# A three-layer transformer block on one core: scans spread over the weight stream, layer norm in eight units, features laid out ahead

## The reference

```python
def conformer_conv(h, w_in, dw, dw_b, ln_g, ln_b, w_out):
    a, b, z = jnp.split(h @ w_in, 3, axis=-1)
    v = a * jax.nn.sigmoid(b)
    v = depthwise_conv(v, dw, 31 taps, pad 15) + dw_b
    v = jax.nn.silu(layer_norm(v, ln_g, ln_b))
    return (v * jax.nn.silu(z)) @ w_out

def hgrn_direction(q, k, v, log_f):          # for each head, state carried over chunks of 64
    b = jnp.cumsum(fb, axis=2)
    decay = jnp.exp(jnp.where(lower_tri, b[t] - b[s], -jnp.inf))
    scores = jnp.einsum("bhtk,bhsk,bhtsk->bhts", qb, kb, decay)
    ...                                      # o_intra + o_inter, new_state

def hgrn2_mixer(h, w_in, lb_fwd, lb_bwd, o_norm, w_out):
    q, a_f, a_b, i, z = jnp.split(h @ w_in, 5, axis=-1)
    # forget(a, lb): log_f = log(lb + (1-lb) sigmoid(a)), key = (1-lb) sigmoid(-a)
    o = rms_norm(forward(q, k_f, i, lf_f) + backward(q, k_b, i, lf_b), o_norm)
    return (o * jax.nn.silu(z)) @ w_out
# x = x + conformer_conv(rms_norm(x)); x = x + hgrn2_mixer(rms_norm(x))
# x = x + sliding_window_attention(rms_norm(x)); x = x + swiglu(rms_norm(x))
```

## Time and profile before

| | us |
|---|---|
| median of 3 runs (2176.8 to 2177.96) | 2177.4 |
| the profiled execution | 2176.5 |
| its span | 2174.7 |
| TensorE busy | 2044.6 (94%) |
| VectorE busy | 1244.8 (57%) |
| ScalarE busy | 1067.7 (49%) |
| GpSimd busy | 241.6 (11%) |
| mean granted TensorE clock | 0.975 |

### The profile page before, as it was taken

One profiled execution on the slowest core, in us unless ns is written; L12 is line 12 of the kernel. 1 busy time (PEld: TensorE's weight loads), 2 busy tenths in 40 slices (PEclk: granted clock), 3 DMA queues, 4 the chain that ended last, 5 costly groups with the idle time before them and its releaser, 6 DMA issues.

```text
span 2174.7 us, 26997 instructions
## 1 busy us (share of the span) xinstructions
PE 2044.6 (94%) x9552; PEld 1687.3 (78%) x9552; DVE 1244.8 (57%) x1678; ACT 1067.7 (49%) x1353; POOL 241.6 (11%) x108
## 2 busy tenths in 40 slices
PE   4999997999898989979999897899999999999999
PEld 4777776888686878868788776788888888888887
DVE  1199975454676857578656663454544454544443
ACT  4444445445656666666455563354444444433332
POOL 3888860000000000000000000000000000000000
PEclk9999999999999999999999997899999999999999
DMA  4665562565344444433556332356656665655654
GB/s 153 187 178 182 177 193 75 167 203 180 121 135 145 137 134 135 146 116 123 183 179 202 97 100 76 123 183 191 191 174 199 194 185 182 195 189 187 190 187 155
DMA packets 182189, 350.71 MB, mean 161 GB/s; under 512 B 11548, under 2 KB 11932, under 8 KB 182044
## 3 DMA queue, kind: packets, MB, share of 16 engines
q1 hardware_dynamic: 180608, 348.17, 51.6%
q10 hardware_dynamic: 1478, 1.23, 0.2%
HBM read 347.26 MB, written 2.10 MB: 161 GB/s over the span
## 4 chain that ended last, share of the span: by engine, by line
PE 84%; DVE 6%; ACT 5%; issue 2%; DVEq 1%; ACTq 1%; DMA 1%; POOL 1%
PE acc L362 25%; PE acc L363 25%; PE acc L364 25%; PE T L477 3%; PE T L344 2%; ACT w_hi L640 1%; DVEq L974 1%; DVE w_lo L982 1%; DMA cy<-in_hgrn_lb_bwd_dram 1%; ACTq L650 1%; PE T L556 1%; POOL w_lo L331 1%; DVE Xc L1113 0%; PE T L565 0%; PE T L567 0%
## 5 line engine op out<-in xcount | busy, mean ns | idle before, releaser
L982 DVE TENSOR_TENSOR w_lo<-raw,w_hi 128x1024 fp32r<-128x1024 f32 x560 | 677.2, 1223 | 655.0 <-ACT w_hi L640 648.5
L640 ACT ACTIVATE w_hi<-raw 128x1024 fp32r<-128x1024 f32 x656 | 683.3, 1058 | 560.5 <-PE acc L364 532.0
L362 PE MATMUL acc<-w_hi,h_hi 128*128 128x512 f32 x1888 | 752.5, 399 | 48.1 <-DVE w_lo L982 36.5
L363 PE MATMUL acc<-w_lo,h_hi 128*128 128x512 f32 x1888 | 741.5, 393 | 0.0
L364 PE MATMUL acc<-w_hi,h_lo 128*128 128x512 f32 x1888 | 740.9, 392 | 0.0
L362 PEld LDWEIGHTS acc<-w_hi,h_hi 128*128 128x128 f32 x1888 | 358.4, 190 | 131.0 <-DVE w_lo L982 40.3
L364 PEld LDWEIGHTS acc<-w_hi,h_lo 128*128 128x128 f32 x1888 | 358.0, 190 | 76.3
L363 PEld LDWEIGHTS acc<-w_lo,h_hi 128*128 128x128 f32 x1888 | 358.5, 190 | 70.9
L331 POOL TENSOR_TENSOR w_lo<-raw,w_hi 128x1024 fp32r<-128x1024 f32 x96 | 228.0, 2400 | 68.8 <-ACT w_hi L640 68.7
L1037 DVE SCALAR_TENSOR_TENSOR T<-vpad,feat,T 128x256 f32<-128x256 f32 x464 | 183.6, 481 | 0.7 <-DVE T L1037 0.7
L362 PE MATMUL acc<-w_hi,y_hi 128*128 128x512 f32 x384 | 159.2, 415 | 20.3 <-DVE y_lo L987 11.3
(11 more groups left out here) (197 smaller groups left out, 1398.0 us busy)
## 6 DMA issues: line engine op xcount, KB each, us to landing
raw<-in_hgrn_w_in_dram SPq DMA_DIRECT2D x160, 512.0 KB, 4.3
raw<-in_conv_w_in_dram SPq DMA_DIRECT2D x96, 512.0 KB, 4.2
raw<-in_ffn_w_gate_dram SPq DMA_DIRECT2D x88, 512.0 KB, 4.4
raw<-in_ffn_w_up_dram SPq DMA_DIRECT2D x88, 512.0 KB, 3.9
raw<-in_ffn_w_down_dram SPq DMA_DIRECT2D x88, 512.0 KB, 4.7
raw<-in_attn_w_qkv_dram SPq DMA_DIRECT2D x40, 512.0 KB, 4.2
raw<-in_conv_w_out_dram SPq DMA_DIRECT2D x32, 512.0 KB, 4.8
raw<-in_hgrn_w_out_dram SPq DMA_DIRECT2D x32, 512.0 KB, 4.7
```

What stands on the lines that cost most here:

```text
L362: nc.tensor.matmul(o, hi[:, kt, a], w_hi[:, slot, kk, :], start=kt == 0, stop=False)
L363: nc.tensor.matmul(o, hi[:, kt, a], w_lo[:, slot, kk, :], start=False, stop=False)
L640: A(w_hi[:, slot, :, :], raw[:, slot, :, :], ACT.Copy).then_inc(hi_ready, 1)
L982: TT(w_lo[:, slot, :, :], raw[:, slot, :, :], rounded(w_hi[:, slot, :, :]), ALU.subtract).then_inc(split_ready, 1)
```

## The change

Three things are changed at once.

1. The feature table and x are also given in a turned layout, channels on partitions. `feat` is one load of 128 rows, and x comes in a second time, turned, as four loads into `xT` (the place of `szt`), each before one of the first four weight loads; the ordinary x is loaded behind them. The turns of features and of x at the start are gone. VectorE instead of GpSimd makes `w_lo` for the first 16 chunks.
2. Layer norm: the taps of both halves of a group use one PSUM bank; the mean is summed in two parts at hooks 14 and 27 of `conv_z`, the variance in four parts at hooks 28 to 31. `z_turn(3)` goes behind the second chunk of `conv_out`. The four units become eight units of two blocks; three are begun at hook 3, the others one per hook at hooks 4 to 9, and TensorE waits for unit c before chunk c.
3. Scan passes: the undecayed level comes first, behind TensorE's chunk 7; the forward scans stand at VectorE's hook 8, the backward ones at 9, the two key operations at 10 and 11, the first differences at 12, and the later differences one chunk behind the weighting before them instead of at once behind it. `turn` of the third projection and `gates` are one or two chunks earlier.

```diff
+FIRST_LOWS = 2 * CPG
...
+            def turned_in(k):
+                sp.dma_start(xT[:, 4 * k:4 * k + 4, :], t["x_turned"][:, 4 * k:4 * k + 4, :]).then_inc(xT_in[k], 16)
...
+            def ab(j):
+                at = Hooks()
+                if is_first(j):
+                    for k in range(4):
+                        at.put(k, lambda k=k: turned_in(k)).put(4 + k, lambda k=k: x_rows_in(k))
...
-            for n in range(ph["conv_out"].chunk0):
+            pool.wait_ge(split_ready, FIRST_LOWS)
+            for n in range(FIRST_LOWS, ph["conv_out"].chunk0):
...
+            def mean(q0, q1):
+                pe.wait_ge(c_tap, q1 * GROUP_TAPS)
+                for kt in range(4 * q0, 4 * q1):
+                    last = nc.tensor.matmul(T[:, 3, 0:S], ones[:, :], cy[:, kt, :], start=kt == 0, stop=kt == KT - 1)
                 last.then_inc(c_mean, 1)
...
+            def variance(q):
+                pe.wait_ge(c_sq, q + 1)
+                for i in range(4):
+                    last = nc.tensor.matmul(T[:, 2, 0:S], ones[:, :],
+                                            (atok, fg)[q % 2].rearrange("p a (b c) -> p (a b) c", c=S)[:, i, :],
+                                            start=q == 0 and i == 0, stop=q == 3 and i == 3)
+                last.then_inc(c_var, 1)
             at = Hooks().put(5, lambda: v_turn(3))
...
+            at.put(14, lambda: mean(0, 3)).put(27, lambda: mean(3, 4))
+            for q in range(4):
+                at.put(28 + q, lambda q=q: variance(q))
             stream("conv_z", 0, h_hi, h_lo, at)
-            z_turn(3)
-            mean()
-            variance()
-            stream("conv_out", 0, y_hi, y_lo, x_turns("conv_out", 1, (c_zc, 8)), lambda c: pe.wait_ge(c_lo, c // 2 + 1))
+            stream("conv_out", 0, y_hi, y_lo, x_turns("conv_out", 1, (c_zc, 8)).put(1, lambda: z_turn(3)),
+                   lambda c: pe.wait_ge(c_lo, c + 1))
...
-                at = Hooks().put(0, lambda: turn(j, 0, qtok)).put(1, lambda: turn(j, 1, aftok)).put(3, lambda: turn(j, 2, abtok))
-                for l in range(9):
-                    at.put(10 + 2 * l, lambda l=l: level(j, l))
+                at = Hooks().put(0, lambda: turn(j, 0, qtok)).put(1, lambda: turn(j, 1, aftok)).put(2, lambda: turn(j, 2, abtok))
+                at.put(7, lambda: level(j, 0))
+                for s in range(1, 9):
+                    at.put(10 + 2 * s, lambda s=s: level(j, s))
...
+            act.dma_start(feat[:, :, :], t["features"]).then_inc(feat_in, 16)
+            act.dma_start(ident[:, :], t["c_ident"]).then_inc(small_in, 16)
...
+            def ln_act(u):
+                act.wait_ge(c_n, u + 1)
+                for kt in (2 * u, 2 * u + 1):
+                    last = A(cy[:, kt, :], cy[:, kt, :], ACT.Silu, scale=feat[:, kt, R_LNG:R_LNG + 1], bias=feat[:, kt, R_LNB:R_LNB + 1])
+                last.then_inc(c_act, 1)
+            def ln_hi(u):
+                act.wait_ge(c_g, u + 1)
+                A(y_hi[:, 2 * u:2 * u + 2, :], cy[:, 2 * u:2 * u + 2, :], ACT.Copy).then_inc(c_hi, 1)
+            def ln_first():
+                ln_root()
+                ln_act(0)
+                ln_act(1)
+                ln_hi(0)
+                ln_act(2)
+                ln_hi(1)
+                z_out(3)
             at = v_steps(3)
...
+            at.put(31, lambda: ln_square(0)).put(31, lambda: ln_square(1))
...
+            at = Hooks().put(0, lambda: ln_square(2)).put(1, lambda: ln_square(3)).put(3, ln_first).put(5, lambda: z_copy(3))
+            for u in range(3, 8):
+                at.put(u + 1, lambda u=u: ln_act(u)).put(u + 1, lambda u=u: ln_hi(u - 1))
+            at.put(9, lambda: ln_hi(7))
...
-                at = Hooks().put(3, lambda: q_copy(j)).put(4, lambda: gates(j, 0)).put(6, lambda: gates(j, 1))
+                at = Hooks().put(3, lambda: q_copy(j)).put(4, lambda: gates(j, 0)).put(5, lambda: gates(j, 1))
                 for d in range(2):
                     at.put(6 + d, lambda d=d: ln_f(j, d)).put(8 + d, lambda d=d: ln_k(j, d))
-                at.put(10, lambda: exp(j, 0))
-                for l in range(ACT_TAKES):
-                    at.put(13 + 2 * l, lambda l=l: take(j, l))
-                for l in range(2, 9):
-                    at.put(11 + 2 * l, lambda l=l: exp(j, l))
+                at.put(10, lambda: take(j, 0))
+                for s in range(1, 9):
+                    at.put(11 + 2 * s, lambda s=s: exp(j, s))
+                    if s < ACT_TAKES:
+                        at.put(13 + 2 * s, lambda s=s: take(j, s))
...
+            def ln_scale(u):
+                TT(unit(u), unit(u), ln_rstd[:, :].unsqueeze(1).to_broadcast([P, 2, S]), ALU.mult).then_inc(c_n, 1)
...
+                ln_scale(0)
+                ln_scale(1)
+                ln_gate(0)
+                ln_scale(2)
+                ln_gate(1)
                 ln_lo(0)
...
+            centre()
+            at = Hooks().put(3, ln_first)
+            for u in range(2, 8):
+                if u < 7:
+                    at.put(u + 2, lambda u=u: ln_scale(u + 1))
+                at.put(u + 2, lambda u=u: ln_gate(u)).put(u + 2, lambda u=u: ln_lo(u))
...
-                at = Hooks().put(2, lambda: bounds_of(j)).put(7, lambda: diagonal(j)).put(9, lambda: scans(j)).put(9, lambda: keys(j)).put(9, lambda: diffs(j, 0))
-                for l in range(9):
-                    if l > ACT_TAKES:
-                        at.put(11 + 2 * l, lambda l=l: take(j, l - 1))
-                    at.put(11 + 2 * l, lambda l=l: weigh(j, l))
-                    if l < 8:
-                        at.put(11 + 2 * l, lambda l=l: diffs(j, l + 1))
+                at = Hooks().put(2, lambda: bounds_of(j)).put(6, lambda: diagonal(j)).put(8, lambda: scan_f(j)).put(9, lambda: scan_b(j))
+                at.put(10, lambda: keys(j, 0)).put(11, lambda: keys(j, 1)).put(12, lambda: diffs(j, 1))
+                for s in range(1, 9):
+                    if s > ACT_TAKES:
+                        at.put(11 + 2 * s, lambda s=s: take(j, s - 1))
+                    at.put(11 + 2 * s, lambda s=s: weigh(j, s))
+                    if s < 8:
+                        at.put(12 + 2 * s, lambda s=s: diffs(j, s + 1))
```

More of the change, by code:

```diff
@@ L186, in build @@
         sg = sb(conv_s, "sg", [P, TB, GC])
-        rows = cy[0:ROWS, 0:8, :].rearrange("p a b -> p (a b)")
+        xT = szt
         ln_std = sb(conv_s, "ln_std", [P, S])
@@ L392, in normed @@
                 return lambda c: pe.wait_ge(n_lo, 4 * s + c // 2 + 1)
-            pe.wait_ge(small_in, 16 * 11)
-            for kt in range(KT):
-                last = nc.tensor.transpose(T[:, 2 + kt // 8, (kt % 8) * ROWS:(kt % 8 + 1) * ROWS],
-                                           rows[:, kt * P:(kt + 1) * P], ident[0:ROWS, 0:ROWS])
-            last.then_inc(feat_T, 1)
-            x_turn(0, 0)
-            pe.wait_ge(feat_ready, 2)
-            x_turn(0, 1)
             def v_turn(j):
+                if is_first(j):
+                    pe.wait_ge(small_in, 16)
                 pe.wait_ge(c_v, j + 1)
@@ L413, in ab @@
                 if is_first(j):
-                    stream("conv_ab", j, h_hi, h_lo, Hooks().put(0, lambda: x_turn(0, 2)).put(1, lambda: x_turn(0, 3)), normed(0))
+                    stream("conv_ab", j, h_hi, h_lo, None, normed(0))
                 else:
@@ L428, in z_turn @@
                 transposes(T01, sg, c_zT)
-            def mean():
-                for half in range(2):
-                    pe.wait_ge(c_tap, 3 * GROUP_TAPS + (half + 1) * HALF_TAPS)
-                    for kt in (range(14), range(14, KT))[half]:
-                        last = nc.tensor.matmul(T[:, 2, 0:S], ones[:, :], cy[:, kt, :], start=kt == 0, stop=kt == KT - 1)
-                last.then_inc(c_mean, 1)
-            def variance():
-                for q in range(4):
-                    pe.wait_ge(c_sq, q + 1)
-                    for i in range(4):
-                        last = nc.tensor.matmul(T[:, 3, 0:S], ones[:, :],
-                                                (atok, sg)[q % 2].rearrange("p a (b c) -> p (a b) c", c=S)[:, i, :],
-                                                start=q == 0 and i == 0, stop=q == 3 and i == 3)
-                    last.then_inc(c_var, 1)
+            def mean(q0, q1):
+                pe.wait_ge(c_tap, q1 * GROUP_TAPS)
+                for kt in range(4 * q0, 4 * q1):
+                    last = nc.tensor.matmul(T[:, 3, 0:S], ones[:, :], cy[:, kt, :], start=kt == 0, stop=kt == KT - 1)
+                last.then_inc(c_mean, 1)
+            def variance(q):
[5 more added lines that the diff above has]
+                last.then_inc(c_var, 1)
             at = Hooks().put(5, lambda: v_turn(3))
@@ L1104, in diagonal, with scan_f, scan_b @@
                                in1=E[:, 1, 1, h, :], op0=ALU.mult, op1=ALU.add)
-                last.then_inc(g_diag, 1)
-            def scans(j):
+                last.then_inc(g_G, 1)
+            def scan_f(j):
```

(4 more changed lines are left out.)

234 lines of the change are left out of this document (106 added, 128 removed).

## The result

| | before | changed |
|---|---|---|
| median | 2177.1 | 2096.4 |
| lowest to highest, 4 runs each | 2176.0 to 2178.0 | 2096.0 to 2101.7 |
| span of the profiled execution | 2174.7 | 2094.5 |
| mean granted clock | 0.975 | 0.984 |

The ratio is 0.9635 (95% interval 0.9619 to 0.9652): 81 us gained, where 59 were forecast. It is as well to see first where the gain lies. Each row of the table is the time from the last use of the stage before's last weight chunk to that of the stage's own, in us, by the semaphore of used chunks. The first `hgrn` loop (88.0 us in both kernels) and the 4.5 us behind the last chunk are left out.

A forecast was written before the change was run, and what follows sets the result against it. TensorE, busy 94% with weight streaming, was taken as the bound, so only its standing or slow running could give time. Start 20 + scans 43 - layer norm 4 = 59 us: 2177.4 to 2118 us, own range 2110 to 2127, wider 2102 to 2136.

The forecast's parts named there:

- Scans: Four scan passes: idle time and low clock recovered, 10.6 us in each of three, 11 in the last; 43 us together.
- the 1 allowed: Each of the first three scan passes: 1 us of idleness expected to stay, taken off the recovered time.
- the 1.8 of the prediction: Scan pass: 1.8 us of low clock to be recovered, nine matmuls at 0.43 instead of 0.23 us.
- That the level comes nearly on time: Scan pass, first decayed level: weighting done at 573.0 us, TensorE arriving at 572.8, so nearly no wait.
- The room of the next ones: Scan pass, later decayed levels: 0.5 to 0.9 us of room, from 7.23 us per level against a 7.1 us chain.
- Start: Kernel start: TensorE begins at about 13.0 instead of 31.86 us; 18.9 + 2 - 1, 20 us gained.
- The landing of 7.1 us: Start: features, identity, a quarter of turned x and first weights, 1.46 MB, landed near 7.1 us.
- Layer norm: Layer norm and following output-weight chunks: 6.9 us gained up to the first chunk, 9.6 lost behind, 1.3 for clock; 4 lost.
- the 2.7 of the prediction: Layer norm: net loss of 2.7 us from the schedule, before the addition for the clock.
- the 1.3 that it added for the clock: Layer norm: 1.3 us more loss, as TensorE is idle two fifths of that stretch.
- The rival of hidden hooks: Layer norm: ScalarE works while VectorE does, gaining 7 to 10 us, 2105 us; chance 0.18 together with a clean scan.
- The low clock through chunks 2 to 7: Layer norm rival: interrupted chunks stay at the low clock, six costing 4 us more, 2122 us; chance 0.05.

The follow-up runs named there:

- the first part alone: The kernel before with only the turned features and x and VectorE's first 16 low parts, without the unused buffers: 2155.7 us, ratio 0.9902.
- the second part alone: The kernel before with only the layer norm change (spread mean and variance, eight units of two blocks), without the unused buffers: 2178.1 us, ratio 1.0005.

## Why the prediction was too high

**What bounds the kernel** was read rightly: TensorE's standings at three places, and each went as its views said. The miss lies in what was left out and in two sizes.

**The buffers: the step that failed**, 10 of the 22 us (9.4 and 11 by the medians, 10.1 by stages). The prediction took it that the pace of streaming, 2.72 us a chunk, holds wherever TensorE is busy, and costed only edits that move instructions. In the down projection the pace was 2.80, and in `conv_out` and `hgrn_out` 2.774, because of where their stationary tiles start. Without the buffers the changed kernel takes 2105.8 us, inside the range. The trace before had the sign, but its means over the whole kernel hide it (399, 393 and 392 ns for `h`, raised by the slow clock, 396 for `f`). A window of the kernel before without waits, 1450 to 1800 us in the up and gate projections, beside the row of 396 ns above, would have asked why:

```profile
L363 PE MATMUL acc<-w_lo,h_hi 128*128 128x512 f32 x506 | 196.8, 389 | 0.0
```

The two declarations were the second hint.

**Scans**, 6 of the 22: mechanism right, two terms too small. The pass was to get back 9.8 us of idleness and 1.8 of low clock and keep 1. The first pass kept 0.3 to 0.4 us of waits for the 1 allowed, and got back 12.4 in all (122.8 to 110.4), so what stood beside the idle time had cost 12.4 + 0.4 - 9.8 = 3.0 us. The slow clock is the 1.8 of the prediction: nine matmuls in the kernel before, from 572.14 us, begin 0.43 us apart, and from 576.02 the pace is full again. The other 1.2 us had no term: four waits, each about 0.3 us dearer than its row. A row of 0.39 us is counted as busy to its end, though the next could begin 0.23 us behind its start (0.16 us), and the second matmul behind a wait begins 0.34 us after the first and not 0.23 (329.32 and 329.66 us in the layer norm). In the last pass 7.4 us were left in and 5.4 remained (waits of 4.4 and 1.0 us). That the level comes nearly on time held. The room of the next ones was told as 0.5 to 0.9 us, while the prediction's own figures, 7.23 against 7.1, leave 0.1; the trace has 0.65 at the second decayed level, whose weighting ends at 556.73 and whose matmuls start at 557.38. (The row's durations add up to 10.5 us and not 10.3, and twice 1.8 is 3.6 and not 3.4; neither changes the miss.)

**Start**, 5 of the 22: the first matmul at 13.14 us for 13.0. (The landing of 7.1 us does not follow from its own terms, 4 + 2.8 = 6.8 us; it was measured at 7.43.) Behind it 3.2 us came in the first 16 chunks for the 1 forecast; 1.6 are two waits for GpSimd's low parts that are gone, the rest was not separated. In the other groups of `conv_ab` 3.3 us came for nothing forecast: two of the three spells of low clock (1.6 us dearer each) are missing there, and one of them stands in `conv_z` instead. This is no firm part of the change. Where such a spell falls varied from kernel to kernel: with the first part alone two stand in `conv_ab`, one in `conv_z` and one early in `conv_out`, and these last two stages, whose steps that part leaves alone, took 3.8 us more than before.

**Layer norm**: 2.5 us lost for 4. By its terms: idle behind the variance 7.5 us for 7.2, wait at the first variance 2.1 for 2.2, and the steps of chunks 98 to 103 above the plain pace 10.7 us for 11.3. The waits under them add up to 8.0 us and not to 11, since the last turn of the gate (0.9 us) lies in the first of these steps and each of them is 0.3 us longer than its wait, as in the scans. The 2.5 us hold two things that are not the schedule's: 1.7 us given by the buffers in `conv_out` and 1.6 us taken by the spell of low clock in `conv_z`. The schedule itself lost 2.5, as the kernel without the buffers shows (220.6 us for 218.1, with no spell in `conv_z`), and 2.0 with the second part alone. That is the 2.7 of the prediction without the 1.3 that it added for the clock, and the 1.3 did not come: the low clock ends within the first chunk, whose matmuls begin 0.43 us apart and then 0.23. The rival of hidden hooks is refuted.

The low clock through chunks 2 to 7 did not come in the changed kernel, yet it is not ruled out for this schedule. With `h_hi` and `h_lo` moved by 32 bytes the same stretch of `conv_out`, whose tiles stand as in the changed kernel, fell to the low clock three times again, for the first time behind a wait of 1.84 us where the changed kernel has one of 1.81 and kept the full clock. Windows of 31 us from about the end of the second chunk, of the changed kernel and of that one (granted clock 1.00 and 0.83):

```profile
326.00:357.00 31.00, 23.03 (x99) 17.30 (x98) 20.93 (x27) 18.41 (x30) 0.00 (x0) 1.00 0.38 119
```

```profile
333.00:364.00 31.00, 24.03 (x85) 18.16 (x85) 18.65 (x25) 15.77 (x25) 0.00 (x0) 0.83 0.33 102
```

`conv_out` took 3.1 us more there (114.7 for 111.6), near the 4 of the rival. The Trainium skill ("TensorE: Matmul & The Clock Gate", Part 1) says that idleness lowers the clock and activity restores it. The traces agree with both; which waits lower it they do not settle.

**The range** was built from the schedule's rivals alone. None of them could go below 2098, and the cause that did was no case in it.

## What to carry to other kernels

Read the mean duration of equal matmuls stage by stage, before any wait: a difference with equal clock and no idleness is a cause of its own, and here 3% of a stage lay in where a tile starts. A unit of work hung between weight chunks should feed as many chunks as the fixed work beside it lasts; make the first units small and the later ones large. A long row on a helping engine is worth splitting at each point where the stream's own work can go between, and the splits, more than the order of the pieces, bring the gain.

## What the hardware showed

- TensorE's pace depends on where its stationary tiles start in SBUF: fp32 matmuls of 128x128 by 128x512 began every 226.7 ns with all tiles on multiples of 128 bytes and every 233.3 ns with all of them 32 or 64 bytes off (234.4 at 96), at the full clock in both. With one of two kinds of tile off, a chunk of twelve took 2.774 us (high parts off, 32 bytes), 2.80 (low parts, 32) and 2.795 (low parts, 96), where 2.720 is the floor. The loads of the stationary tiles do not show it in their own rows: 188 ns in either case.
- A scan pass with four waits of 9.8 us in all, the longest 7.8, cost 3.0 us beyond them: 1.8 of slow clock behind the longest and about 0.3 at each wait. The waits of the interrupted chunks (1.8 us once, 1.4 four times, 0.45 once) left the clock at 1.00 in the changed kernel; in the run with `h_hi` moved, the waits there (1.84, 2.57 and 2.56 us) stood beside three spells at 0.50.
- TensorE's first matmuls in the changed kernel, from 13.14 us on, begin 0.43 us apart for 5.7 us, the pace of 1.2 GHz, 2.7 us dearer than at the full one. The windows view shows 1.00 there, but the trace has no entry of the granted clock before 18.9 us, where the matmuls speed up, and a window without an entry reads 1.00. The 1.00 of the earlier trace rows, by which the prediction went, says as little: the first entry of that trace stands at 29.7 us. The Trainium skill ("TensorE: Matmul & The Clock Gate", Part 1) has the array start slow, and the matmuls agree with it:

```profile
15.01 0.63 PE L377 MATMUL acc<-w_lo,h_hi 128*128 128x512 f32 x1
15.44 0.63 PE L378 MATMUL acc<-w_hi,h_lo 128*128 128x512 f32 x1
```

```profile
12.00:16.00 4.00, 2.86 (x7) 2.28 (x8) 4.00 (x9) 4.00 (x10) 0.00 (x0) 1.00 1.03 387
```
